# Reordering the preparation of the RWKV mixer in a two-layer decoder trunk: exponentials ahead of the gates, lora products around the last attention outputs

## The reference, cut to what matters

```
h = RMSNorm(x);  P = h @ W_in
y_A = HGRN2(P_A)   y_B = DSA(P_B)   y_C = RWKV7(P_C)   y_D = FoX(P_D)
m = sum_n sigmoid(P_gate_n) * (y_n @ W_branch_n)
x = x + RMSNorm(m @ W_out)
x = x + RMSNorm(relu(RMSNorm(x) @ W_up)^2 @ W_down)
```

```
xm = p + (prev - p) * mu;   r, k, v, w_in, a_in, g_in = split(xm)
w_log = -softplus(-(w0 + tanh(w_in) @ w2)) - 0.5;  decay = exp(-exp(w_log))
a = sigmoid(a0 + a_in @ a2);   g = sigmoid(g_in) @ g2
v = v + (v_first - v) * sigmoid(v0 + (v @ v1) @ v2)        # second layer only
kk = k * k_k;  kk = kk * rsqrt(max(sum(kk*kk), 1e-24))
k = k * (1 + (a - 1) * k_a)
```

## Time and profile before

| | |
|---|---|
| median of 3 runs | 2180.81 us (2171.2 to 2186.48) |
| profiled execution | 2169.13 us |
| its span | 2167.3 us |
| TensorE busy | 2039.5 us, 94% of the span |
| VectorE, ScalarE, GpSimd busy | 43%, 36%, 46% |
| granted clock of TensorE, mean | 0.976 of full speed |

### The profile page before, as it was taken

The page is one execution under the profiler, slowest core; times in us unless marked ns, Lnnn a source line. Parts: engine busy times, 40 slices in busy tenths (PEclk is TensorE's granted clock), DMA queues, the critical chain, the costliest instruction groups (busy, mean ns, idle before and its releaser), DMA issues.

```text
span 2167.3 us, 31573 instructions
## 1 busy us (share of the span) xinstructions
PE 2039.5 (94%) x10760; PEld 1602.6 (74%) x10760; DVE 924.7 (43%) x1674; ACT 780.2 (36%) x1196; POOL 1003.2 (46%) x1231
## 2 busy tenths in 40 slices
PE   7999998999999899999899999989999979999995
PEld 5876756877777688888678776567776768888884
DVE  5737955223232513223277478543233225133143
ACT  6334254223443522222363343541244343222224
POOL 4444423212647555557534444322144675455574
PEclk9999989999999999999999999999999999999997
DMA  4222211001222232223212222110021222222232
GB/s 168 69 79 71 86 40 39 30 31 33 85 69 88 78 97 96 94 95 95 86 56 82 85 72 75 44 37 29 30 69 49 88 78 87 95 95 96 92 99 96
DMA packets 50352, 161.72 MB, mean 75 GB/s; under 512 B 5280, under 2 KB 13600, under 8 KB 49952
## 3 DMA queue, kind: packets, MB, share of 16 engines
q1 hardware_dynamic: 49056, 157.05, 22.1%
q10 hardware_dynamic: 1152, 2.86, 0.4%
HBM read 157.79 MB, written 2.10 MB: 74 GB/s over the span
## 4 chain that ended last, share of the span: by engine, by line
issue 54%; POOL 41%; PE 3%; POOLq 1%; DVE 1%; DMA 0%; ACT 0%; SPq 0%; DVEq 0%; ACTq 0%
POOL w_lo L1432 21%; POOL w_lo L1462 16%; POOL slab L1452 2%; PE bank L553 1%; PE bank L554 1%; PE bank L555 1%; POOL rstd L1441 1%; POOL slab L1473 1%; POOLq L1459 0%; POOL slab L1455 0%; DMA w_raw<-wproj 0%; POOLq L1428 0%; DVE u_lo L1531 0%; DVE u_hi L1542 0%; DVE u_lo L1543 0%
## 5 line engine op out<-in xcount | busy, mean ns | idle before, releaser
L1432 POOL TENSOR_TENSOR w_lo<-w_raw,w_hi 128x256 fp32r<-128x256 f32 x624 | 498.7, 831 | 810.8 <-ACT w_hi L1056 810.4
L553 PE MATMUL bank<-hn_hi,w_hi 128*128 128x512 f32 x1312 | 549.5, 419 | 24.0 <-DVE hn_lo L1531 17.3
L1462 POOL TENSOR_TENSOR w_lo<-w_raw,w_hi 128x256 fp32r<-128x256 f32 x512 | 380.8, 776 | 302.0 <-ACT w_hi L1392 302.0
L555 PE MATMUL bank<-hn_hi,w_lo 128*128 128x512 f32 x1312 | 518.0, 395 | 0.0
L554 PE MATMUL bank<-hn_lo,w_hi 128*128 128x512 f32 x1312 | 517.6, 395 | 0.0
L553 PEld LDWEIGHTS bank<-hn_hi,w_hi 128*128 128x128 f32 x1312 | 250.2, 191 | 104.4 <-issue 28.2
L553 PE MATMUL bank<-u_hi,w_hi 128*128 128x512 f32 x736 | 297.2, 404 | 24.0 <-POOL w_lo L1424 11.5
L1392 ACT ACTIVATE w_hi<-w_raw 128x1024 fp32r<-128x1024 f32 x128 | 135.8, 1061 | 430.7 <-DMA w_raw<-wrest 406.0
L555 PEld LDWEIGHTS bank<-hn_hi,w_lo 128*128 128x128 f32 x1312 | 249.6, 190 | 54.2
L555 PE MATMUL bank<-u_hi,w_lo 128*128 128x512 f32 x736 | 287.6, 391 | 0.0
L554 PE MATMUL bank<-u_lo,w_hi 128*128 128x512 f32 x736 | 287.6, 391 | 0.0
(11 more groups left out here) (314 smaller groups left out, 2705.2 us busy)
## 6 DMA issues: line engine op xcount, KB each, us to landing
w_raw<-wrest SPq DMA_DIRECT2D x144, 512.0 KB, 3.3
w_raw<-wmerge SPq DMA_DIRECT2D x80, 512.0 KB, 3.6
w_raw<-wproj SPq DMA_DIRECT2D x64, 512.0 KB, 3.4
x<-x_in SPq DMA_DIRECT2D x4, 512.0 KB, 7.1
slab<-rope ACTq DMA_DIRECT2D x2, 1024.0 KB, 4.9
out<-x SPq DMA_DIRECT2D x4, 512.0 KB, 2.6
con<-tables SPq DMA_DIRECT2D x1, 898.0 KB, 11.0
slab<-masks SPq DMA_DIRECT2D x1, 896.0 KB, 12.7
```

Source lines behind the costliest of these rows:

```text
L553: mm(o_, stat[0], mov[0], start=first, stop=False)
L555: return mm(o_, stat[1], mov[0], start=False, stop=last)
L1432: ins = pool.tensor_tensor(wlo[:, s_, cs], wraw[:, s_, cs], whi[:, s_, cs].bitcast(f32), SUB)
L1462: ins = pool.tensor_tensor(wlo[:, s_, cs], wraw[:, s_, cs], whi[:, s_, cs].bitcast(f32), SUB)
```

## The change

Places in `schedule()`: the last round of the top-k gets four dense steps more, and the second place of the preparation 13 instead of 15. The limit at the end of gate1,3 stays, so the last places of the attention and place "C" find nothing left to do.

TensorE: lora products 0 and 1 are issued before the last attention outputs, directly behind transpose 15. `dense("C")` comes behind the value products.

ScalarE: Tanh alone (with the signal to TensorE) stands between transposes 14 and 15; the Sigmoid comes behind transpose 15. The squares come behind the fourth lora eviction, the take of "C" behind the value gates. The exponentials, the norm factor and the copy of the value stand ahead of the takes of "c_start" and "c_prep 0", with one chunk split (that of gate1,6) between the exponentials and the norm factor.

VectorE: branch1,0 and branch1,1 are emptied before it waits for the value gates instead of behind the norm's clamp, and up to the whole of REACH.

The products of the levels are the same in both kernels.

```diff
-        place(("b_topk", r), FILL["b_topk"][r // 8], ("gate1", 3))
+        place(("b_topk", r), FILL["b_topk"][r // 8] + 4 * (r == TOPK // 8 - 1), ("gate1", 3))
...
-        "b_att": ((1, 1), (1, 0)), "c_start": 4, "c_prep": (16, 15), ...
+        "b_att": ((1, 1), (1, 0)), "c_start": 4, "c_prep": (16, 13), ...
 TensorE
                         transposed(2 * p + 1)
                         dense(("bd"[which] + "_att", 2 * p + 1, 1))
+                    if which == 0:
+                        pe.wait_ge(*c_act.at(L, 1))
+                        pe.wait_ge(*par_loaded.at(L, 32))
+                        pe.wait_ge(*at_mx.at(L, 16))
+                        lora_out(0, 4)
+                        lora_out(1, 5)
                     outputs(7)
...
-                pe.wait_ge(*c_act.at(L, 1))
-                pe.wait_ge(*par_loaded.at(L, 32))
-                pe.wait_ge(*at_mx.at(L, 16))
-                lora_out(0, 4)
-                lora_out(1, 5)
                 pe.wait_ge(*at_pt.at(L, 16))
                 lora_out(2, 6)
-                dense("C")
                 pe.wait_ge(*c_sg.at(L, 1))
                 lora_out(3, 4)
...
                 ins.then_inc(*c_vh.up())
+                dense("C")
                 dense("c_start")
 ScalarE
                         elif which == 0:
-                            lora_hidden()
+                            act.wait_ge(*c_mix.at(L, 1))
+                            fn(S(15, 0)[0:32, :], S(15, 0)[0:32, :], ACT.Tanh).then_inc(*c_act.up())
...
+                    if which == 0:
+                        fn(S(15, 0)[64:128, :], S(15, 0)[64:128, :], ACT.Sigmoid)
                     take_steps(REACH[("bd"[which] + "_att", 15, 1)])
...
-                for t in range(FT):
-                    fn(S(5, t), S(13, t), ACT.Square, scale=pcol("kk", t)).then_inc(*c_sq.up())
-                take("C")
                 lora_taken(3, 4)
                 act.wait_ge(*c_vh.at(L, 1))
                 fn(S(11, 0)[0:32, :], ps[5][0:32, :], ACT.Copy).then_inc(*c_vhc.up())
                 for t in range(FT):
-                    fn(S(4, t), S(13, t), ACT.Copy, scale=pcol("kk", t))
+                    fn(S(5, t), S(13, t), ACT.Square, scale=pcol("kk", t)).then_inc(*c_sq.up())
                 for t in range(FT):
                     act.wait_ge(*c_vg.at(L, t + 1))
                     fn(S(6, t), ps[6 + t][:, :], ACT.Sigmoid, bias=pcol("v0", t)).then_inc(*c_vgs.up())
+                take("C")
+                for t in range(FT):
+                    fn(S(4, t), S(13, t), ACT.Copy, scale=pcol("kk", t))
...
-                take("c_start")
-                take(("c_prep", 0))
                 act.preload_act_table(ACT.Ln)
                 act.wait_ge(*c_ex.at(L, 1))
...
+                split_to(INDEX[("branch1", 3)] + 1)
                 act.wait_ge(*c_kkv.at(L, 1))
...
                 fn(v1st[:, :, :].rearrange("p t n -> p (t n)"), slab[:, 14, :], ACT.Copy)
+                take("c_start")
+                take(("c_prep", 0))
                 take(("c_prep", 1))
 VectorE
                 link(tt(col[:, 4, :], end, mid, SUB))
+                gated_to(REACH["c_start"])
                 dve.wait_ge(*c_vgs.at(L, 2))
...
                 ins.then_inc(*c_kkv.up())
-                gated("c_start")
                 dve.wait_ge(*c_kf.at(L, 1))
```

More of the change, by code:

```diff
@@ L164 @@
 FILL = {"a_level": (8, 8, 8, 8, 8, 8, 8, 8), "a_keys": 2, "a_chunk": 2, "a_norm": 4, "b_rope": (8, 4, 4, 3, 3, 3, 3), "b_ix": 1, "b_topk": (5, 6),
-        "b_att": ((1, 1), (1, 0)), "c_start": 4, "c_prep": (16, 15), "c_mask": 1, "c_level": (1, 1), "c_out": (1, 1, 1), "c_norm": 4,
+        "b_att": ((1, 1), (1, 0)), "c_start": 4, "c_prep": (16, 13), "c_mask": 1, "c_level": (1, 1), "c_out": (1, 1, 1), "c_norm": 4,
         "d_prep": 20, "d_att": (1, 1)}
@@ L689, in attention, with lora_out @@
                         dense(("bd"[which] + "_att", 2 * p + 1, 1))
-                    outputs(7)
+                    if which == 0:
[4 more added lines that the diff above has]
+                        lora_out(1, 5)
+                    outputs(7)
+                def lora_out(i_, b):
+                    lo = i_ // FT * 32
+                    t = i_ % FT
+                    mm(ps[b][:, :], lora[lo:lo + 32, t * P:(t + 1) * P], S(15, 0)[lo:lo + 32, :], start=True, stop=True)\
+                        .then_inc(*c_lw.up())
                 enter()
@@ L797, in _ @@
                 attention(0, S(8), S(9), slab[:, 10, :].rearrange("p (c n) -> p c n", c=NT), 0)
-                pe.wait_ge(*c_act.at(L, 1))
-                pe.wait_ge(*par_loaded.at(L, 32))
-                pe.wait_ge(*at_mx.at(L, 16))
-                def lora_out(i_, b):
-                    lo = i_ // FT * 32
-                    t = i_ % FT
-                    mm(ps[b][:, :], lora[lo:lo + 32, t * P:(t + 1) * P], S(15, 0)[lo:lo + 32, :], start=True, stop=True)\
-                        .then_inc(*c_lw.up())
-                lora_out(0, 4)
-                lora_out(1, 5)
                 pe.wait_ge(*at_pt.at(L, 16))
                 lora_out(2, 6)
-                dense("C")
                 pe.wait_ge(*c_sg.at(L, 1))
@@ L1182, in attention @@
                         transposed(2 * p + 1)
+                    if which == 0:
+                        fn(S(15, 0)[64:128, :], S(15, 0)[64:128, :], ACT.Sigmoid)
                     take_steps(REACH[("bd"[which] + "_att", 15, 1)])
                     attn_out(which, NT - 1)
-                def lora_hidden():
-                    act.wait_ge(*c_mix.at(L, 1))
-                    fn(S(15, 0)[0:32, :], S(15, 0)[0:32, :], ACT.Tanh)
-                    fn(S(15, 0)[64:128, :], S(15, 0)[64:128, :], ACT.Sigmoid).then_inc(*c_act.up())
                 def attn_out(which, b):
```

## The result

The changed kernel takes 2195.99 us in the median (2173.78 to 2200.22, 20 runs) against 2173.12 for the kernel before, run beside it (2167.75 to 2191.74, 20 runs): **0.8% slower, ratio 1.0077 [1.0053, 1.0101]** (the medians lie 1.1% apart). Medians and ranges here hold all executions, while a ratio leaves out those more than 1.5% above the fastest of their kernel (two of e1's, one of e4's, four of e6's, two of e15's). Forecast were 2161 us and at most 2177. The profiled execution took 2198.78 us, its span is 2196.9 us, its mean granted clock 0.958, where before had 2167.3 us and 0.976.

The account below looks back on a forecast made before the run. TensorE, busy 94% of the span, bounds the kernel through waits and lower clock. Gains of 8.4 and 14.25 us plus 0.3 per layer's attention, less 2.5 per layer for clock, plus 1.7, gave 2180.8 - 20 = 2161 us; range 2147 to 2177.

Parts of the forecast that it names:

- Top-k hole: TensorE's 3.70 us idle at the first logits, until VectorE's top-k ends; 2.7 us of dense steps leave it near 1 us.
- Attention: From the first logits to the lora products: 0.3 us gained per layer, between -0.5 and +1.5.
- The new wait: Ahead of lora product 3, TensorE idles 2.95 us until ScalarE's queue empties the first lora bank.
- Dense work resumes: Behind lora product 3, value products, value gates and sums, dense steps start again at 320.65 us in layer 0.
- Waits on branch1,0 and on the operands' last product gone: TensorE's waits before gate1,4 (2.6 us) and at the first transpose (5.4 us), in each layer, vanish.
- gate1,7's low part: Before the transposes, GpSimd's low weight part takes 4.66 us; TensorE waits 2.4 us for it (bounds 0.5 and 3.5).
- that rival: At gate1,7's low part, GpSimd is blocked for whole VectorE products: 2.9 us later, a gain of 12.5 in all; 5%.
- The sum up to the transposes: First logits to first transposes take 81.5 us per layer; 18.3 us gained, attention's 0.3 and 2.5 clock loss per layer included.
- The step that failed: In the levels, behind the transposes: nothing else moves, same products, one step at each place, same lags.
- The slower rival: Half clock from 311 us to the transposes, up to 29 us more per layer: +35, 2216 us; 7%.
- The table loads: ScalarE's loads cost 1.28 us each; the skill's 2.66 us with drain would leave a gain of 8.7, given 3%.

Follow-up runs that it names:

- e1: The changed kernel with 15 instead of 13 dense steps at the second place of the preparation: 2167.24 us, ratio 0.9959.
- e4: The changed kernel with two dense steps instead of one at both mask places of chunks 2 and 3: 2166.28 us, ratio 0.9969.
- e6: The changed kernel with two additional dense steps instead of four ahead of the attention, at the top-k's last round: 2187.24 us, ratio 0.9992.
- e15: The changed kernel with eight dense steps instead of one in chunk 2, level 2: 2206.48 us, ratio 1.0067.
- e2: The kernel before with only the second preparation place changed, 13 dense steps instead of 15: 2185.16 us, ratio 1.0079.
- e17: The changed kernel with two dense steps instead of one at the second mask place alone, chunks 1 to 3: 2154.47 us, ratio 0.9909.
- e18: The changed kernel with 12 steps at the second preparation place and two at the second mask place of chunks 1 to 3: 2155.67 us, ratio 0.9895.
- e14: The kernel before with four idle identity copies on VectorE at the start of chunk 2 in each layer: 2196.55 us, ratio 1.0091.
- e16: The changed kernel with 12 steps at the second preparation place and two at both mask places of chunks 1 to 3: 2147.39 us, ratio 0.9871.

## Why the prediction was wrong, point by point

- **Top-k hole**: right. 3.70 us became 1.00.
- **Attention**: lora product 0 starts 42.5 us behind step 278 (304.32 - 261.79); laid out were 42.4.
- **The new wait**: right in place and cause, 2.16 us for 2.95. ScalarE's queue of table load, Sigmoid, gates and split was as listed; lora product 3 came 48.7 us behind step 278, laid out were 48.6.
- **Dense work resumes** 59.6 us behind step 278, 57.8 laid out. The 1.8 us are the half clock behind the new wait (311 to 316 us), for which the sum held 2.5 per layer. This term was near.
- **Waits on branch1,0 and on the operands' last product gone**: right. The transposes follow their step without a wait on VectorE.
- **gate1,7's low part**: right that it would be late next, mis-sized: 3.78 us instead of 2.4, outside the bound of 3.5. The merges were taken at the 6.0 us of the earlier trace rows and took 8.0, because VectorE's chain now ran beside them; I had applied the slowdown to the low part alone. VectorE's chain paid too: operands 84.1 us behind step 278 instead of 79.4. The Trainium skill (SBUF — State Buffer, "SBUF: two separate sides") has the loser of the port blocked for the whole instruction. Here both engines' instructions stretch at the same time, VectorE's to 1.8 times, GpSimd's to 1.3 times their length; two engines that took turns would show that too, so the trace doesn't decide on the rule. The gain up to the transposes fell nearer to that rival's 12.5 us than to mine, for another reason.
- **The sum up to the transposes**: 97.15 + 91.3 - 2 x 86.2 - 2 x 1.4 = 13.3 us, clock included, for 18.3. A shortfall of 5 us. In layer 0 the stretch is 4.7 us longer than the 81.5 laid out: 1.8 by the dip behind the new wait (2.5 were set aside for it), 1.4 by the longer wait on the low part, 0.7 by the half clock behind that (345 to 353 us), and 0.8 by small distances between steps.
- **The step that failed**: "Behind the transposes nothing else moves: the levels keep their products and one step at each place, with the same lags." The products and the steps at each place did stay; the waits did not, and the clock did not. The end of each dense unit moved by two steps against the chunk starts, and with it a gate product and GpSimd's low parts came onto VectorE's masks. The first waits of chunks 1 to 3 grew from 0.48 us to 1.36, 1.01 and 1.01, and behind them came half clock, 44 us of loss in the two layers of the profiled execution and 25.8 us in the mean of the runs, for which the sum had no term. I had counted the two missing steps as 1.4 us paid later; they cost the kernel before 0.8% by themselves (e2).
- **The slower rival** named the right mechanism, half clock held for tens of us, and the wrong place: in the preparation half clock lasted 5 and 8 us (311 to 316, 345 to 353). My reason for 7% was that "dense steps ended every one within 5 us". That was read from places where dense steps come in a row; in the levels they come singly, half clock held for up to 36 us, and the earlier trace rows had no row from there. Whether the single steps are what lets it hold is not shown (e15). With a gain of 13 in hand, one stretch of 17 us is enough to lose it.
- **The table loads**: 1.28 us each, with the next activation right behind (323.36, 324.65, 325.95). The Trainium skill (ScalarE: Activation LUTs, "What ACT_TABLE_LOAD costs") adds a drain of the engine to each; the trace does not agree, there is no gap between the loads and the activations.

What stays open: what ends a stretch in the levels; what decides, among chunk starts with the same pair of waits, whether the clock falls in a given execution; and whether the kernel before's own slower executions (its lost clock ranges from 48 to 79 us) are of the same kind, since no profile shows one.

## What to carry to other kernels

A step moved out of one place is paid where it is missing, but it also shifts the end of every unit behind it; look at what those ends set off (evictions, weight splits) and onto which short wait of TensorE they fall. Price TensorE's waits by what stands behind them: 2 us of wait ahead of the lora products and dense steps cost about 2 more in clock; 2 us in two pieces, ahead of narrow products with single dense steps, cost nothing at some starts and 17 at others, so judge such a kernel by many executions. If two short waits follow each other, one covered may do: e17 covers the second alone. And when a change gains where it should and the whole is slower, read the granted clock and the number of products per stretch ahead of all else, since busy time looks better, not worse.

## What the runs showed of the hardware that was not expected

- Half clock (0.50 of full speed, the 1.2 GHz level) held for 34 us while TensorE was busy for 33.6 of them, with 64-column products and single dense steps. With the same kind of work it also ended after 11 us (492 to 503 in the changed kernel, 453 to 464 in e6).
- Two waits of 1.0 and 0.9 us, 2.5 us apart, came before a fall at 19 of 44 starts; with the second at 0.36 us or less none of 40 starts had one, eight of which had a first wait of 1.0 to 1.36 us (e17, e18). One wait of 2.3 us was enough alone at both starts that had it (e14).
- Execution times come in clusters some 20 us apart, as whole stretches would make them (not shown, one execution of each kernel was profiled): e2's twelve runs are seven at 2180 to 2186 us and five at 2203 to 2205. The median of a kernel that is liable to the fall therefore says little: e6 spreads over 43 us, e16, with its starts covered, over 4.
- VectorE's 128x1024 products take 1.22 us in quiet and 2.2 to 2.3 beside GpSimd's merges, which take 2.0 us each instead of 1.5.
